# Issuing the DRAM weight sums of both layers earlier in a two-layer attention kernel

## The chip, the cores and the metric

The kernel runs on one core of a Trainium2 chip. The metric is the device time of one execution in microseconds, the median of the runs. The core has TensorE (matrix products), VectorE, ScalarE, GpSimd (called Pool below) and SyncE, each with its own in-order stream of instructions; they meet at semaphores. SyncE and Pool also issue DMA transfers, which run on the core's 16 DMA engines.

## The reference

Two transformer layers in a row, on 512 tokens of width 1024 and 16 meta tokens, in float32. Layer one:

```
proj  = rms_norm(h) @ w_in            # queries, keys, values, latent, index keys, gates
o_a   = sliding-window attention with sinks (8 heads)
o_b   = latent attention: an indexer picks the top 128 keys of each token,
        softmax over them, bias by distance
h    += (sigmoid(gate_a) * (o_a @ w_branch_a) + sigmoid(gate_b) * (o_b @ w_branch_b)) @ w_out
h    += (silu(rms_norm(h) @ w_gate) * (rms_norm(h) @ w_up)) @ w_down      # width 2816
```

Layer two has the same frame; its attentions are a differential attention (4 heads of two softmax maps each) and a windowed attention with grouped keys and sinks. A final rms_norm gives the 512 output rows.

## The kernel before, in words

Every large product is taken in three passes: a weight tile (1024 x 128, 512 KB) is loaded by SyncE into one of two `stage` buffers, ScalarE rounds it to `wh` (L918), and VectorE or Pool subtracts to get the low half `wl` (Pool: `low`, L746); TensorE then multiplies high by high, high by low and low by high. TensorE waits for the low half of a tile before its first product (in `product` and `gate_quarters`), and SyncE loads the next tile into a buffer only when its low half is made.

The work stands in a fixed order on each engine. The stages (`PHASES`) are, in layer one: `kv1`, `bq1`, `iq1`, `aq1`, `uq1` (keys and query weights), `gates1` woven with the window attention and the top-k selection, latent attention, `br1`, `out1`, and the feed-forward in three parts a, b and c: gate/up products `gu1a` (from about 375 us), down products `dn1a` (456), `gu1b` (500), `dn1b` (567), `gu1c` (600), `dn1c` (680). In layer two: `kv2` (730), `qa2`, `qb2`, the differential attention (to 884), `gates2` woven with the window attention, `br2`, `out2`, and the same three feed-forward parts (`gu2a` ends near 1199).

Part of the gate/up products uses a scheme with fewer multiplications: it needs, beside the weights themselves, sums of quarters of the weight matrices. These sums are made in DRAM by Pool's DMAs. `sum_dmas` issues them: for each of the three parts of a layer 16 transfers, the first 8 plain copies (L769), the next 8 accumulating (L771, `accum_op=ALU.add`), of which 8 to 11 take from the weights and 12 to 15 from the sums. A transfer is 512 KB in part a, 768 KB in b, 1024 KB in c. All count on one semaphore, `sums_in`. SyncE waits for a whole part at L672 and then loads the sums (`wsum`) beside the weights.

Before the change Pool issued them so. In `gates1`, two after the low halves of each of 8 pairs of weights (`SUMS_AT[1]`), all of part a. In latent attention, one after every fourth of 32 masks (`mask_bias`, which may run four masks ahead of VectorE), the 8 copies of part b. Then `feed_sums(1)`: when the last mixed tile of layer one is there (`mix_ok`), the accumulates of b and all of part c, each after the landing of the one before. In layer two: one after every second of Pool's 14 steps in the differential attention (`stack_maps_meta`, which copies the meta columns of a map into `m8d`, where TensorE turns them after each 4 maps), copies of part a; one to three after each pair of `gates2`; the rest in `feed_sums(2)`. A wait for the landing of all transfers before stood ahead of steps 0, 8, 12 and 14 of part a and step 0 of part b, and from step 8 of part b on ahead of every transfer; in latent attention and in the differential attention none of them but the first could stop Pool.

Lines that the steps below touch: Pool's waits and copies between the stages (L792 to L904), TensorE's turn of `m8d` (L2529), its gate products (L2520), VectorE's use of a mask (L1697), the ordinary products (L2293) and those with sums (L2316).

## Time and profile before

| | us |
|---|---|
| median of 3 runs | 1472.45 (1471.33 to 1475.7) |
| profiled execution, its own time | 1473.38 |
| its span, first to last instruction | 1471.7 |
| TensorE busy | 1452.7 |
| VectorE / ScalarE / Pool busy | 975.2 / 654.3 / 258.2 |
| mean granted TensorE clock | 0.997 |

A row of a timeline gives the start in us from the span's start, the duration, the engine, the line and the tiles; what stands in brackets is how long the engine was idle before it and what released it. A Pool row with DMA_DIRECT2D is the time in which Pool issues a transfer, not that in which it runs. "DMA to landing" is the time from the issue to the last byte. The clock is TensorE's granted clock as a share of 2.4 GHz.

### The profile page before, as it was taken

The numbers are of one execution on the slowest core, as the hardware profiler recorded it, in microseconds if no ns is written. First come the engines' busy times: TensorE is split into PE (matmuls) and PEld (weight loads), VectorE is DVE, ScalarE is ACT, GpSimd is POOL, SyncE is SP. The second block draws the span as 40 slices with busy tenths as digits, with TensorE's granted clock in tenths as the row PEclk, the third lists the DMA queues.
The fourth block names the chain that finished last, engine by engine and source line by source line (L and its number), as shares of the span: only waits on it lengthen the run. The fifth ranks groups of instructions, "written<-read, shape, count | busy, mean of one in ns | idle before, by whom it ended". The sixth has DMA issues, their size and how long they took to land.

```text
span 1471.7 us, 23871 instructions
## 1 busy us (share of the span) xinstructions
PE 1452.7 (99%) x8712; PEld 1253.2 (85%) x8712; DVE 975.2 (66%) x1779; ACT 654.3 (44%) x1175; POOL 258.2 (18%) x260
## 2 busy tenths in 40 slices
PE   9999999999999999999999999999999999999998
PEld 8868786888898898999899777777888988989997
DVE  6678977575776576787744372434767765867875
ACT  5234446535453353465411373544344533534643
POOL 2024536201101100000003675331011001000000
PEclk9999999999999999999999999999999999999999
DMA  7536674249899993663223237653388999736632
GB/s 187 148 100 211 173 133 130 79 111 191 202 328 226 250 217 98 199 184 106 86 86 86 58 101 162 151 188 80 107 186 226 305 218 242 213 95 195 185 104 93
DMA packets 342909, 236.91 MB, mean 161 GB/s; under 512 B 24729, under 2 KB 322837, under 8 KB 342814
## 3 DMA queue, kind: packets, MB, share of 16 engines
q1 hardware_dynamic: 305518, 152.24, 36.4%
q0 software_dynamic: 37216, 83.27, 24.8%
q8 instruction: 60, 0.98, 0.3%
q14 instruction: 35, 0.29, 0.1%
q10 hardware_dynamic: 80, 0.14, 0.0%
HBM read 233.48 MB, written 81.88 MB: 214 GB/s over the span
## 4 chain that ended last, share of the span: by engine, by line
PE 88%; DMA 6%; DVE 3%; ACT 1%; issue 1%; DVEq 0%; SPq 0%; POOL 0%; ACTq 0%
PE psL L2293 37%; PE psL L2520 12%; PE psS L2316 10%; PE psL L2316 6%; PE psS L2293 5%; PE psT L2316 4%; PE psT L2529 2%; DMA stage<-in_w_ffn_up 1%; DMA stage<-in_w_ffn_gate 1%; DMA stage<-in_w_ff_up 1%; PE psL L2655 1%; PE psS L2836 1%; PE psS L2570 1%; PE psL L2791 1%; PE psS L2814 1%
## 5 line engine op out<-in xcount | busy, mean ns | idle before, releaser
L918 ACT ACTIVATE wh<-stage 128x1024 fp32r<-128x1024 f32 (+3 forms) x211 | 203.6, 965 | 362.1 <-PE psL L2293 199.6
L1398 DVE TENSOR_TENSOR wl<-stage,wh 128x1024 fp32r<-128x1024 f32 (+2 forms) x168 | 183.8, 1094 | 57.7 <-ACT wh L918 57.3
L2293 PE MATMUL psL<-hid,wh 128*128 128x512 f32 x672 | 207.3, 390 | 0.0
L2520 PE MATMUL psL<-hn,wh 128*128 128x512 f32 x496 | 165.0, 414 | 0.8 <-DVE yn L2176 0.8
L2293 PE MATMUL psL<-hn,wh 128*128 128x512 f32 x528 | 165.0, 394 | 0.0
L2293 PEld LDWEIGHTS psL<-hid,wh 128*128 128x128 f32 x672 | 125.6, 188 | 26.2 <-DVE wl L1398 0.6
L2293 PE MATMUL psL<-hid,wl 128*128 128x512 f32 x336 | 130.7, 389 | 0.0
L746 POOL TENSOR_TENSOR wl<-stage,wh 128x1024 fp32r<-128x1024 f32 (+1 forms) x43 | 97.7, 2273 | 172.7 <-ACT wh L918 172.7
L2293 PEld LDWEIGHTS psL<-hn,wh 128*128 128x128 f32 x528 | 97.7, 188 | 23.1 <-issue 3.3
L2520 PEld LDWEIGHTS psL<-hn,wh 128*128 128x128 f32 x496 | 84.5, 189 | 24.5 <-issue 11.1
L2293 PE MATMUL psL<-hn,wl 128*128 128x512 f32 x264 | 102.9, 390 | 0.0
L1901 DVE TENSOR_TENSOR wsl<-wsum,wsh 128x1024 fp32r<-128x1024 f32 x72 | 88.2, 1224 | 22.3 <-ACT wsh L1166 21.4
L2520 PE MATMUL psL<-hn,wl 128*128 128x512 f32 x248 | 97.8, 394 | 0.0
L2316 PE MATMUL psS<-xt,wsh 128*128 128x256 f32 x432 | 80.2, 283 | 0.8 <-ACT part_x L1226 0.8
L2293 PE MATMUL psL<-mix,wh 128*128 128x512 f32 x256 | 79.9, 393 | 0.8 <-DVE wl L1814 0.8
L2293 PE MATMUL psS<-hn,wh 128*128 128x264 f32 x416 | 78.5, 290 | 0.9 <-DVE hn L1845 0.5
L1166 ACT ACTIVATE wsh<-wsum 128x1024 fp32r<-128x1024 f32 x72 | 75.4, 1048 | 5.6 <-DMA wsum<-weight_sums_1g 1.9
L2293 PEld LDWEIGHTS psL<-hid,wl 128*128 128x128 f32 x336 | 63.1, 188 | 13.2
L2028 DVE TENSOR_TENSOR ft<-psL,Rk 128x512 f32<-128x512 f32 x46 | 31.8, 691 | 62.4 <-PE psL L2293 62.4
L2316 PEld LDWEIGHTS psS<-xt,wsh 128*128 128x128 f32 x432 | 67.4, 192 | 1.0 <-ACT part_x L1226 1.0
L2293 PEld LDWEIGHTS psS<-hn,wh 128*128 128x128 f32 x416 | 65.7, 192 | 2.6 <-issue 1.2
L2316 PE MATMUL psS<-xt,wsl 128*128 128x256 f32 x216 | 61.1, 283 | 0.0
(507 smaller groups left out, 3333.0 us busy)
## 6 DMA issues: line engine op xcount, KB each, us to landing
stage<-in_w_in SPq DMA_DIRECT2D x53, 512.0 KB, 4.0
wsum<-weight_sums_1g SPq DMA_DIRECT2D x18, 512.0 KB, 5.2
wsum<-weight_sums_1u SPq DMA_DIRECT2D x18, 512.0 KB, 5.3
wsum<-weight_sums_2g SPq DMA_DIRECT2D x18, 512.0 KB, 4.7
wsum<-weight_sums_2u SPq DMA_DIRECT2D x18, 512.0 KB, 4.5
stage<-in_w_out SPq DMA_DIRECT2D x16, 512.0 KB, 4.7
stage<-in_w_ffn_down SPq DMA_DIRECT2D x32, 256.0 KB, 3.0
stage<-in_w_ff_down SPq DMA_DIRECT2D x32, 256.0 KB, 3.0
```

The lines of the kernel that those rows point to most:

```text
L746: pool.tensor_tensor(wl[:, b, 0:n], stage[:, b, 0:n], wh[:, b, 0:n].bitcast(F32), ALU.subtract).then_inc(lo[b], 1)
L918: act.activation(wh[:, b, 0:n], stage[:, b, 0:n], ACT.Copy).then_inc(hi[b], 1)
L1166: act.activation(wsh[:, cols], wsum[:, cols], ACT.Copy).then_inc(ws_hi, 1)
L1398: v.tensor_tensor(wl[:, b, 0:n], stage[:, b, 0:n], wh[:, b, 0:n].bitcast(F32), ALU.subtract).then_inc(lo[b], 1)
L1901: v.tensor_tensor(wsl[:, cols], wsum[:, cols], wsh[:, cols].bitcast(F32), ALU.subtract).then_inc(ws_lo, 1)
L2028: v.tensor_tensor(ft[:, 2 * b, :], psL[:, b, :], R, ALU.mult).then_inc(upper_ok, 1)
L2293: ins = pe.matmul(dst, w[:, b, k * P:(k + 1) * P], x[:, part, k, c0:c1], start=done_ + n == 0, stop=done_ == kc - 1 and n == 2)
L2316: ins = pe.matmul(dst, w[:, cols], x(part, k), start=not add and k + n == 0, stop=k == KD // 2 - 1 and n == 2, skip_group_check=True)
L2520: ins = pe.matmul(psL[:, b, :], w[:, b, k * P:(k + 1) * P], hn[:, part_, k, META:], start=k + n == 0, stop=k == KD - 1 and n == 2)
L2529: ins = pe.transpose(psT[:, n % 2, m * P:(m + 1) * P], tile[:, col:col + P], ident[:])
L2570: ins = pe.matmul(psS[:, 2 * (i % 2) + 1, h * HD:(h + 1) * HD], PTa[:, u % 2, n * P:(n + 1) * P], avn[:, c, h // 4 * HD:h // 4 * HD + HD], ...
L2655: ins = pe.matmul(psL[:, i % 2, h * HD:(h + 1) * HD], PT[:, n % 4, m * P:(m + 1) * P], vB[:, c, h * HD:(h + 1) * HD], start=h == 0 and m = ...
```

## The change

The same 96 transfers are issued, in the same order and with the same sizes, at other places of Pool's stream. `sum_dmas(l, first, last, one_by_one)` now takes numbers 0 to 47 that run over the three parts of a layer. With `one_by_one` it waits before each transfer for the landing of all before it; without, only before steps 0, 8, 12 and 14 of a part. The places:

- layer one: 0 to 6 one by one behind the transfer of the window bias, ahead of the copy into `cm8`; 7 to 25 in `gates1`; 26 to 31 one by one in latent attention, behind masks 1, 6, 11, 16, 21 and 26; 32 to 47 in `feed_sums(1)`;
- layer two: 0 to 7 one by one when TensorE has reached `dn1b`, 8 to 15 when it has reached `dn1c`; 16 to 21 one by one in `kv2`, behind the `iota`; 22 to 29 one by one in the differential attention; 30 to 42 in `gates2`; 43 to 47 in `feed_sums(2)`.

```diff
--- before.py
+++ after.py
@@ -145,7 +145,7 @@
 SUM_DMAS = 16
-SUMS_AT = {1: (0, 2, 4, 6, 8, 10, 12, 14, 16), 2: (8, 10, 12, 14, 16, 19, 22, 24, 26)}
+SUMS_AT = {1: (7, 10, 12, 14, 16, 19, 22, 24, 26), 2: (30, 32, 34, 36, 38, 40, 41, 42, 43)}
 PHASES = [("kv1", 4, KD, 1), ("bq1", 2, KD, 1), ("iq1", 2, KD, 1), ("aq1", 4, KD, 2), ("uq1", 4, 2, 1),
@@ -749,28 +749,27 @@
                 low(name, i, 0)
                 low(name, i, 1)
-            def sum_dmas(l, part, first, last):
-
-                before = SUM_DMAS * (3 * l - 3 + part)
-                t0, t1 = summed_pairs(part)
-                cols = slice(t0 * P, t1 * P)
-                second = slice((FPAIRS + t0) * P, (FPAIRS + t1) * P)
-                upper, lower = slice(0, D // 2), slice(D // 2, D)
+            def sum_dmas(l, first, last, one_by_one=False):
+
                 for n in range(first, last):
-                    if before + n and (n in (0, 8, 12, 14) or 16 * part + n >= 24):
-                        pool.wait_ge(sums_in, 16 * (before + n))
-                    m = "gu"[n % 2]
+                    before = SUM_DMAS * len(FPARTS) * (l - 1) + n
+                    part, step = divmod(n, SUM_DMAS)
+                    t0, t1 = summed_pairs(part)
+                    cols = slice(t0 * P, t1 * P)
+                    second = slice((FPAIRS + t0) * P, (FPAIRS + t1) * P)
+                    upper, lower = slice(0, D // 2), slice(D // 2, D)
+                    if before and (one_by_one or step in (0, 8, 12, 14)):
+                        pool.wait_ge(sums_in, 16 * before)
+                    m = "gu"[step % 2]
                     w, s12, s43 = w_ffn[l, m], w_sums[l, m, 0], w_sums[l, m, 1]
                     to, src = ((s12[upper, cols], w[upper, second]), (s43[lower, cols], w[upper, cols]),
                                (s12[lower, cols], w[lower, second]), (s43[upper, cols], w[lower, cols]),
                                (s12[upper, cols], w[lower, second]), (s43[lower, cols], w[upper, second]),
-                               (s12[lower, cols], s43[lower, cols]), (s43[upper, cols], s12[lower, cols]))[n // 2]
-                    if n < 8:
+                               (s12[lower, cols], s43[lower, cols]), (s43[upper, cols], s12[lower, cols]))[step // 2]
+                    if step < 8:
                         pool.dma_start(to, src).then_inc(sums_in, 16)
                     else:
                         pool.dma_start(to, src, accum_op=ALU.add).then_inc(sums_in, 16)
-
-
             def copies(row, dram, length, h0, h1):
@@ -789,6 +788,7 @@
             copies(fA_row, fA_dram, LEN_A, 0, NH)
             pool.wait_ge(f_out, 16)
             windows(fA_dram, LEN_A, biasA, NEAR, 0, NH, biasA_in)
+            sum_dmas(1, 0, SUMS_AT[1][0], one_by_one=True)
             pool.wait_ge(key_taken, 2)
             pool.tensor_copy(cm8[:], cT[:, 0:META].unsqueeze(1).broadcast_to([P, NH, META])).then_inc(cm8_ok, 1)
             low_pair("uq1", 0)
@@ -803,7 +803,7 @@
                     low("gates1", i, 1)
                 else:
                     low_pair("gates1", i)
-                sum_dmas(1, 0, SUMS_AT[1][i], SUMS_AT[1][i + 1])
+                sum_dmas(1, SUMS_AT[1][i], SUMS_AT[1][i + 1])
             def mask_bias(j):
@@ -813,11 +813,10 @@
                     pool.wait_ge(ph["la"]["neg"], j - 3)
                 pool.tensor_tensor(biasM[:, j % 4, 0:K], biasB[:, h, NKEY - K:NKEY], selm[:, i, 0:K], ALU.subtract).then_inc(biasM_ok, 1)
-            def feed_sums(l):
+            def feed_sums(l, first):
                 pool.wait_ge(mix_ok, KD * l)
-                sum_dmas(l, 1, 8 if l == 1 else 10, SUM_DMAS)
-                sum_dmas(l, 2, 0, SUM_DMAS)
+                sum_dmas(l, first, SUM_DMAS * len(FPARTS), one_by_one=True)
             la_units = list(latent_units())
             for b in range(2):
@@ -825,15 +824,20 @@
             pool.wait_ge(biasB_in, 4 * 16)
             for j in range(len(la_units)):
                 mask_bias(j)
-                if j % 4 == 3:
-                    sum_dmas(1, 1, j // 4, j // 4 + 1)
-
-            feed_sums(1)
+                if j % 5 == 1 and j < 30:
+                    sum_dmas(1, SUMS_AT[1][-1] + j // 5, SUMS_AT[1][-1] + j // 5 + 1, one_by_one=True)
+
+            feed_sums(1, SUMS_AT[1][-1] + 6)
+            pool.wait_ge(mm[0], PAIR0["dn1b"])
+            sum_dmas(2, 0, 8, one_by_one=True)
+            pool.wait_ge(mm[0], PAIR0["dn1c"])
+            sum_dmas(2, 8, 16, one_by_one=True)
             pool.wait_ge(ev[1], PAIR0["kv2"] + 1)
             pool.memset(m8d[:, :, 4 * META:], 0.0).then_inc(zeros, 1)
             pool.iota(dist[:], pattern=[[-1, DIST]], base=3 * P, channel_multiplier=1,
                       allow_small_or_imprecise_dtypes=True).then_inc(dist_ok, 1)
+            sum_dmas(2, 16, 22, one_by_one=True)
             def bias_unit(j):
@@ -893,13 +897,12 @@
                 else:
                     bias_window(u - 8, u - 7)
                 if u % 2 == 0:
-                    sum_dmas(2, 0, u // 2 - 1, u // 2)
-            sum_dmas(2, 0, 7, 8)
+                    sum_dmas(2, 21 + u // 2, 22 + u // 2, one_by_one=True)
+            sum_dmas(2, 29, 30, one_by_one=True)
             for i in range(PAIRS["gates2"]):
                 low_pair("gates2", i)
-                part = SUMS_AT[2][i] // SUM_DMAS
-                sum_dmas(2, part, SUMS_AT[2][i] - part * SUM_DMAS, SUMS_AT[2][i + 1] - part * SUM_DMAS)
-            feed_sums(2)
+                sum_dmas(2, SUMS_AT[2][i], SUMS_AT[2][i + 1])
+            feed_sums(2, SUMS_AT[2][-1])
         @block.scalar
```

## Rows read from the trace of the kernel before

**Rows 1.** The page, part 1: engine, busy us (share of the span), instructions.

```profile
PE 1452.7 (99%) x8712; PEld 1253.2 (85%) x8712; DVE 975.2 (66%) x1779; ACT 654.3 (44%) x1175; POOL 258.2 (18%) x260
```

**Rows 2.** Windows: stretch, length, then busy us (instructions) by engine, clock, DMA share, GB/s.

```profile
416.00:456.00 40.00, 40.00 (x336) 40.00 (x334) 30.12 (x42) 22.54 (x39) 3.55 (x5) 1.00 0.95 297
500.00:542.00 42.00, 37.79 (x298) 37.18 (x297) 27.02 (x36) 20.95 (x35) 2.95 (x3) 0.96 1.04 248
1157.00:1199.00 42.00, 40.77 (x336) 40.17 (x335) 29.87 (x42) 22.14 (x38) 4.33 (x5) 1.00 1.00 257
```

**Rows 3.** Windows: the stretch behind TensorE's gap.

```profile
516.00:520.00 4.00, 3.67 (x18) 3.68 (x19) 3.90 (x5) 2.80 (x7) 0.00 (x0) 0.57 1.04 175
```

**Rows 4.** Chain of waits, 500 to 545: start us, us, what.

```profile
513.36 11.18 DMA stage<-in_w_ffn_gate
```

**Rows 5.** Timeline of Pool, 40 to 110: start, us, operation, idle before it.

```profile
43.14 0.94 POOL L783 DMA_DIRECT2D biasA<-bias_by_distance_A  x1 [9.38 <-DMA bias_by_distance_A<-bias_row_A]
77.52 0.29 POOL L793 COPY cm<-cT 128x128 f32<-128x128 f32 x1 [33.44 <-DVE ikz L1624]
...
104.16 0.65 POOL L769 DMA_DIRECT2D weight_sums_1g<-in_w_ffn_gate  x1
...
108.39 2.40 POOL L746 TENSOR_TENSOR wl<-stage,wh 128x1024 fp32r<-128x1024 f32 x1 [2.24 <-ACT wh L918]
```

**Rows 6.** Timeline of TensorE: gate product of the second pair of weights.

```profile
115.20 0.73 PE L2520 MATMUL psL<-hn,wh 128*128 128x512 f32 x2
```

**Rows 7.** Line 769, the copies, all 48: time from issue to landing.

```profile
DMA to landing us min/median/max: 4.0/5.6/10.0
```

**Rows 8.** Line 771, the accumulates: all 48, then one in 1010 to 1020.

```profile
DMA to landing us min/median/max: 6.6/8.8/12.3
...
L771 POOL DMA_DIRECT2D weight_sums_2u<-in_w_ff_up x1: 1023/1023/1023, 1015.2 to 1015.2; - x1
...
DMA to landing us min/median/max: 7.0/7.0/7.0
```

**Rows 9.** Timeline of Pool and VectorE in latent attention: masks, then the use of mask 27.

```profile
231.72 0.88 POOL L814 TENSOR_TENSOR biasM<-biasB,selm 128x144 f32<-128x144 f32 x2 [6.62 <-DVE negm L1697]
...
264.16 0.70 DVE L1697 CUSTOM_DVE_ANT_0 W<-psS,biasM 128x528 f32<-128x528 f32 x1
```

**Rows 10.** Timeline of Pool, 320 to 530: first sum transfers of each kind, and the last.

```profile
327.69 1.05 POOL L771 DMA_DIRECT2D weight_sums_1g<-in_w_ffn_gate  x1 [60.38 <-DVE mix L1822]
...
396.07 0.66 POOL L769 DMA_DIRECT2D weight_sums_1g<-in_w_ffn_gate  x1 [8.89 <-DMA weight_sums_1u<-weight_sums_1u]
...
452.18 1.04 POOL L771 DMA_DIRECT2D weight_sums_1g<-in_w_ffn_gate  x1 [6.96 <-DMA weight_sums_1u<-in_w_ffn_up]
...
491.12 1.01 POOL L771 DMA_DIRECT2D weight_sums_1g<-weight_sums_1g  x1 [9.48 <-DMA weight_sums_1u<-in_w_ffn_up]
...
524.66 1.01 POOL L771 DMA_DIRECT2D weight_sums_1u<-weight_sums_1u  x1 [11.60 <-DMA weight_sums_1g<-weight_sums_1g]
```

**Rows 11.** Timeline of Pool in layer two's key products.

```profile
777.94 1.00 POOL L861 COPY vm<-vaT 128x512 f32<-128x512 f32 x1 [34.24 <-DVE vaT L1549]
```

**Rows 12.** Timeline of Pool, end of the differential attention.

```profile
856.29 0.68 POOL L769 DMA_DIRECT2D weight_sums_2g<-in_w_ff_gate  x1
...
880.36 0.21 POOL L852 COPY m8d<-W 128x16 f32<-128x16 f32 x1
...
881.64 0.68 POOL L769 DMA_DIRECT2D weight_sums_2u<-in_w_ff_up  x1
882.34 4.71 POOL L746 TENSOR_TENSOR wl<-stage,wh 128x1024 fp32r<-128x1024 f32 x2
```

**Rows 13.** Timeline of TensorE there: last meta turn, first gate product.

```profile
881.32 0.27 PE L2529 MATMUL psT<-ident,m8d 128*128 128x128 f32 x1
...
884.81 0.70 PE L2520 MATMUL psL<-hn,wh 128*128 128x512 f32 x2 [0.80 <-DVE yn L2176]
```

## The prediction

> **What bounds the kernel now.** I read the page's busy shares first: TensorE is busy for 1452.7 of 1471.7 us [rows 1], so only 19 us of the span is open to a gain, and every microsecond for which TensorE is made to wait is added whole. Then I asked, in windows, where these 19 us lie and whether the moved transfers have to do with them. In 500 to 542 TensorE is busy for 37.8 of 42 us, with a mean clock of 0.96; in 416 to 456, where gate and up products of the same kind run, it is busy throughout, and in 1157 to 1199 it is idle for 1.2 us [rows 2]. The chain of waits in the bad stretch runs over the weight loads: one took 11.2 us from issue to landing [rows 4], and a load and the split behind it have to fit the 10.08 us in which TensorE does half a pair. The Pool timeline says what is different there: from 491.12 on Pool has accumulating transfers in flight, in 416 to 456 plain copies [rows 10]. So accumulates beside gate/up products cost 4.2 us of idle time, and 4 us at clock 0.57 that followed the 2.2 us gap (4 x 0.43 = 1.7 us) [rows 3]: 5.9 us in layer one, 1.2 in layer two. That is all that an earlier start can win directly.
>
> **The change, part by part.** A layer has 48 sum transfers, numbered 0 to 47 here: three parts of 16, in each 8 copies and then 8 accumulates, of 512, 768 and 1024 KB by part. Nothing is added or removed; what changes is when Pool issues each, and where it first waits for the landing of the one before (`one_by_one`). Pool is one in-order engine, so behind such a wait stand its other duties: low halves of weights, masks, stacked meta columns.
>
> *Query weights (0 to 6, before the copy into cm8).* Copies land in 4.0 us at best, 5.6 in the median [rows 7]. Pool is free at 44.1 and has nothing else to do until 77.52 [rows 5]. The first queues behind the bias window transfer, say to 50.6; five more at 4.6 make the seventh issue fall at 73.6. It is hidden; at 5.6 it falls at 78.6, and the low half that counts comes only 6 us after 77.52, so it stays hidden. Cost 0, upper end 2.
>
> *Gates of layer one (7 to 25).* Number 8 waits for 7, which is issued at 104.16. With 4.6 to land, two accumulate issues (1.0 and 1.1) and the bias copy, the next low half starts at about 111.2 instead of 108.39 [rows 5], and is ready at 113.6. TensorE wants it at 115.20 [rows 6]: hidden with 1.6 us to spare. The other waits in this loop are for transfers issued a whole pair, 15 us, earlier. Cost 0, upper end 2.
>
> *Latent attention (26 to 31, 768 KB accumulates).* The price of one accumulate is the heart of this forecast. All 48 of them took 6.6 us at least and 8.8 in the median; the one of this size that ran beside little else took 7.0 [rows 8]. I take 7.0, plus 0.2 to the next issue: a cycle c of 7.2. Number 27 goes out at its natural place, about 232.2 [rows 9]; 28, 29, 30 and 31 follow at c each, the last at 261.0. Its issue (1.0) and the mask of unit 27 (1.2) end at 263.2, and VectorE wants this mask at 264.16 [rows 9]. Hidden by 1.0 us: cost 0. In general it is 4c - 29.8, which is 2.2 us at c = 8.0 and 5.4 at 8.8. The four masks that Pool may run ahead are the cover, and here they are nearly used up.
>
> *Layer one's feed (32 to 47, 1024 KB).* It now starts at 327.7, where mix_ok comes, not at 396.07 [rows 10]. By the rows the 8 copies take 56.1 us, the 4 accumulates from the weights 9.7 each (452.18 to 491.12), the 4 from the sums 11.2 each (491.12 to 524.66 is three). That gives copies to 384, accumulates to 423 and then to 467. So the dear accumulates no longer lie beside the second gate/up stage, but they lie beside the whole of the first one, 416 to 456, with the same loads. The 5.9 us go away in 500 to 542 and come back at 416 to 456. Net 0; the ends are -5.9 (they don't come back) and +3 (some cushion less).
>
> *Layer two's part a (0 to 15) in layer one's down products, and 16 to 21 in the key products.* Copies from 566.7 and accumulates from 680, 512 KB, one at a time, beside loads that leave half of the queues' time free; accumulates end near 738. Pool next stands idle for 34.24 us before 777.94 [rows 11], and six copies need under 34. Cost 0, upper end 1.
>
> *Differential attention of layer two (22 to 29).* Here the old program issued copies without a wait. Now 24 to 29 are 768 KB accumulates, and each waits for the one before. 24 goes out at 856.29 as before [rows 12]; 25 at 863.5, 26 at 870.7, 27 at 877.9, 28 at 885.1, 29 at 892.3. Before, the last was issued at 881.64. Two duties stand behind these waits. The last meta column (880.36 before [rows 12]) comes after 28, at 886.3, and TensorE turns it at 881.32 [rows 13]: a wait of 5.0 us. Then follow 3.5 us of work to 889.8. The low half of the first gate weights starts at 893.3 and is ready 2.4 later [rows 12], at 895.7; TensorE wanted it at 884.81 [rows 13]. Both waits together: 10.9 us. Nothing covers them, since TensorE's order is fixed. After the second wait I add one fall of the clock as in [rows 3], 1.7 us (after the first it is hidden in the second wait). Bounds: with c = 6.8 it is 8.9, with 9.0 it is 19.9; the clock 0 to 3.4.
>
> *Gates and out products of layer two (30 to 47).* Two issues a pair, as before; only five accumulates are left for the feed, so they are done before 1157, and the 1.2 us there [rows 2] are won.
>
> Sum: 10.9 + 1.7 + 0 - 1.2 = +11.4 us. The profiled execution took 1473.38 us (span 1471.7), so it becomes 1484.8; it lies 0.9 above the median of the runs, hence 1484 for the median.
>
> The Trainium skill ("DMA: Bandwidth & Descriptors", section "Anatomy of one DMA — SWDGE (gpsimd) path") puts a transfer issued from GpSimd at about 2.0 us and its bytes over 436 GB/s, 3.8 us for 768 KB. If accumulates obeyed that, no wait would reach TensorE at all. The rows say 7.0 us for such an accumulate [rows 8], so the trace does not bear the rule out for accumulates, though it comes near for copies (4.0 at best [rows 7]).
>
> **The rivals.**
> *A: the accumulates leave layer one's gate/up stages unharmed.* For it: the feed starts 68 us earlier, and if accumulates run faster beside the out products, part of them is over before 416. Against it: 134 us of transfers from 327.7 end after 456 in any case. Full effect -5.9: 1478.
> *B: the cycle is longer, 8.0 us.* For it: the median of 8.8 [rows 8]. Against it: few weight loads run in 846 to 895. Then 5 x 0.8 = 4 us more at the gates and 2.2 us in latent attention: 1490.
> *C: an earlier wait surfaces* in the query weights or at the first gates, where the margins are 1.6 to 6 us: about 3 us more, and a fall of the clock: 1489.
> *D, not slower: accumulates that wait for one another land as fast as copies,* since each has the queues to itself. For it: all accumulates of 512 KB were issued in twos. The point from which it decides: c at most 5.0 (856.3 + 5c + 1.0 + 2.4 under 884.8). Then the gates wait for nothing, the feed is over by about 440, and -1.2 and some 3 of the 5.9 us are won: 1468. Against it: the row of 7.0 us had the queue to itself too, and the minimum of 48 is 6.6.
>
> **How the numbers follow.** My forecast 0.58, A 0.18, B 0.13, C 0.05, D 0.06. The time is the forecast's, 1484. Downwards the range takes in A, 1477; upwards B and a little, 1492. A measurement tells about 0.3% (4.4 us) from no change. Only D is faster (0.04; in a weak form it is no change, 0.02), and A together with a cheap cycle comes to no change with 0.02. That leaves 0.92 for slower.
>
> **What would show it.** Right: Pool's issues 7.2 us apart from 856 on, the last at about 892; TensorE idle for 5 us before its last turn of m8d and again before its first gate product, with a fall of the clock behind it; the same idle pattern as in 500 to 542 now in 416 to 460, and none in 500 to 542 or 1170 to 1210. Wrong: accumulates under 5 us, or idle TensorE in the latent stretch 240 to 270, or at 105 to 116.

## The result and the profile after

The changed kernel takes 1494.51 us (median of 4 runs, 1492.79 to 1494.8) against 1472.08 for the kernel before on the same chip: the ratio is 1.0155, with an interval of 1.0135 to 1.0175. So it is slower by about 22 us where 11.4 were forecast, and it lies above the range. Its profiled execution took 1492.79 us, with a span of 1491.0 us against 1471.7: 19.3 us to explain. The busy shares after:

```profile
PE 1457.9 (98%) x8712; PEld 1255.7 (84%) x8712; DVE 980.1 (66%) x1779; ACT 655.6 (44%) x1175; POOL 258.6 (17%) x260
```

TensorE's idle time rose by only 14.1 us [rows 1]; the rest is the clock. To find where the time went I took each of the 8712 products in both traces and asked how much later it starts, counted from the span's start. All kernels here issue the same products in the same order, so this can be done for each; the marks are times of the kernel before:

```
us later at mark    40   222   262   416   460   500   546   740   880   890   925  1157  1200  1450
changed            0.3   0.3   7.4   7.1  10.3  10.3   3.8   2.2   2.6  16.5  21.5  21.4  19.4  19.4
e1 layer one       2.9   2.9   8.9   8.8   9.2   9.2   2.7   2.6   2.7   2.7   2.7   2.7   2.0   4.7
e2 layer two      -0.2  -0.2  -0.2   0.5   0.5   0.5  -3.7  -5.3  -5.1  11.4  11.4  11.2   9.1   9.1
e3                 2.6   2.6   5.0   5.6   9.2   9.2   2.7   1.2   1.6  15.9  17.0  17.7  15.7  15.7
e4                 1.0   1.0   7.8   7.9  11.2  11.2   4.8   4.8   4.8   8.8  14.8  14.7  12.7  12.7
e5                 1.2   1.2   8.4   8.4  11.4  11.4   5.0   3.4   3.4   9.4   9.5  10.1   8.1   8.1
e6                 0.1   0.1   7.1   7.0   8.7   8.8   2.3   4.1   4.6  18.8  23.4  23.5  21.5  21.4
e7                 2.9   2.9   2.6   2.2   5.0   5.0  -1.5  -1.5  -1.5  -1.8   3.5   4.6   2.5   2.5
e8                 0.8   0.7   7.9   7.8   8.4   8.4   1.9   1.9   2.1  10.0  10.1  10.1   8.1   8.1
e9                -0.1  -0.1  -0.3  -0.6   1.4   1.4  -5.1  -5.2  -5.1  -5.4  -5.4  -5.2  -4.9  -4.9
e10                0.0   0.0   7.3   7.1  10.0  10.0   3.5   1.9   2.7  16.5  16.6  16.8  14.8  14.8
e11                2.4   2.4   2.2   1.8   1.8   1.8   0.4   1.2   2.9  18.4  18.4  19.1  17.1  17.1
e12                1.4   1.3   1.1  12.0  12.0  12.0   5.5   7.1   7.1   6.8   6.8   7.8   9.5   9.4
e13                1.2   8.8  15.4  15.1  17.4  17.4  10.9  12.4  13.2  27.3  28.5  29.2  27.1  27.1
e14                0.2   1.8   8.1   7.9   8.3   8.3   1.8   1.8   1.9  16.8  18.1  17.8  15.8  15.8
```

What stands at mark 40 differs from one execution to the next and lies ahead of every moved transfer. For the changed kernel the steps are: **+7.1 in latent attention (222 to 262), +3.2 in gu1a, -6.5 in gu1b (500 to 546), -1.6 before 740, +13.9 at the end of the differential attention (880 to 890), +5.0 in the first gates of layer two (890 to 925), -2.0 before 1200**. The first and the sixth were not in the forecast. Nor was the -1.6, and it is not the change's: the kernel before runs at a mean clock of 0.57 in 731 to 735, and the changed one at 1.00 in the same stage.

```profile
731.00:735.00 4.00, 4.00 (x22) 4.00 (x22) 3.38 (x21) 1.06 (x1) 0.00 (x0) 0.57 0.42 126
...
733.00:737.00 4.00, 4.00 (x36) 4.00 (x36) 2.62 (x16) 0.65 (x1) 0.00 (x0) 1.00 0.45 131
```

The kernels whose transfers of layer two's part a and in the key products stand as in the changed one range from -1.6 to +1.8 between 546 and 740.

**Latent attention.** Pool's timeline there, the accumulates 27 to 31 and two rows of masks (start, us, operation, idle before):

```profile
234.76 1.01 POOL L772 DMA_DIRECT2D weight_sums_1u<-in_w_ffn_up  x1
...
242.23 1.01 POOL L772 DMA_DIRECT2D weight_sums_1g<-weight_sums_1g  x1 [2.83 <-DMA weight_sums_1u<-in_w_ffn_up]
...
249.76 1.01 POOL L772 DMA_DIRECT2D weight_sums_1u<-weight_sums_1u  x1 [2.95 <-DMA weight_sums_1g<-weight_sums_1g]
250.43 4.88 POOL L814 TENSOR_TENSOR biasM<-biasB,selm 128x400 f32<-128x400 f32 x5
257.10 1.01 POOL L772 DMA_DIRECT2D weight_sums_1g<-weight_sums_1g  x1 [1.80 <-DMA weight_sums_1u<-weight_sums_1u]
```

VectorE's rows in the kernel before (masks 16 and 17), then VectorE's and TensorE's in the changed one:

```profile
248.44 0.57 DVE L1697 CUSTOM_DVE_ANT_0 W<-psS,biasM 128x400 f32<-128x400 f32 x1
...
248.93 0.57 DVE L1697 CUSTOM_DVE_ANT_0 W<-psS,biasM 128x400 f32<-128x400 f32 x1
```

```profile
244.09 0.44 DVE L1700 CUSTOM_DVE_ANT_0 W<-psS,biasM 128x272 f32<-128x272 f32 x1 [2.61 <-POOL biasM L814]
...
248.75 0.56 DVE L1700 CUSTOM_DVE_ANT_0 W<-psS,biasM 128x400 f32<-128x400 f32 x1
251.86 0.57 DVE L1700 CUSTOM_DVE_ANT_0 W<-psS,biasM 128x400 f32<-128x400 f32 x1 [2.54 <-PE psS L2631]
```

```profile
255.48 0.47 PE L2532 MATMUL psT<-ident,m 128*128 128x128 f32 x1 [3.90 <-DVE m L1774]
```

Masks 12 to 16 stand behind the wait for 27's landing, and VectorE waits for mask 12 until 244.09; this was still made up for. Masks 17 to 21 stand behind that for 28's, so 17 is begun only at 250.43. VectorE uses 16 at 248.75 and 17 at 251.86; in the kernel before they followed one another, at 248.44 and 248.93. The row names `psS` as the releaser, but what has moved is the mask, which ended at about 251.4. TensorE stands for 3.90 us and then runs at a lower clock, as the windows show (stretch, length, busy us of TensorE, its weight loads, VectorE, ScalarE and Pool, clock, DMA share, GB/s):

```profile
252.00:262.00 10.00, 6.52 (x29) 5.06 (x30) 6.68 (x16) 4.17 (x12) 7.58 (x9) 0.66 0.79 122
255.50:261.50 6.00, 6.00 (x25) 4.54 (x25) 2.88 (x11) 2.78 (x8) 3.78 (x4) 0.50 0.60 82
416.00:460.00 44.00, 42.30 (x319) 40.30 (x317) 30.49 (x41) 22.29 (x36) 5.02 (x5) 1.00 1.11 263
500.00:546.00 46.00, 46.00 (x346) 44.29 (x346) 34.24 (x45) 23.73 (x38) 0.00 (x0) 1.00 0.63 184
...
896.00:902.00 6.00, 2.36 (x6) 1.93 (x7) 0.00 (x0) 0.00 (x0) 5.77 (x3) 0.53 0.73 110
...
899.60:903.20 3.60, 3.56 (x9) 2.85 (x10) 0.00 (x0) 0.00 (x0) 2.25 (x1) 0.50 1.15 221
912.00:925.00 13.00, 9.90 (x42) 7.46 (x41) 6.38 (x7) 3.96 (x10) 6.36 (x4) 0.87 0.84 206
1157.00:1199.00 42.00, 42.00 (x269) 38.37 (x268) 32.68 (x43) 21.80 (x33) 0.00 (x0) 1.00 0.56 161
```

In 252 to 262 the mean clock is 0.66, but part of that lies in the idle time. Behind the wait, in 255.5 to 261.5, TensorE is busy throughout at half its clock (1.2 GHz), so about 3.0 us are lost to the clock beside the 3.9 us of the wait; the kernel before was busy there throughout. The windows of 416 and 500 answer to [rows 2]: gu1a idles for 1.7 us where it idled for nothing, gu1b no longer idles. The last: gu2a has no gap left.

**End of the differential attention and first gates of layer two.** Pool's timeline (the transfers are 24 to 31 and 33; L772 accumulates, L770 copies):

```profile
858.49 1.09 POOL L772 DMA_DIRECT2D weight_sums_2g<-in_w_ff_gate  x1
...
865.93 1.08 POOL L772 DMA_DIRECT2D weight_sums_2u<-in_w_ff_up  x1 [0.81 <-DMA weight_sums_2g<-in_w_ff_gate]
...
873.49 1.06 POOL L772 DMA_DIRECT2D weight_sums_2g<-in_w_ff_gate  x1 [2.87 <-DMA weight_sums_2u<-in_w_ff_up]
...
881.17 1.06 POOL L772 DMA_DIRECT2D weight_sums_2u<-in_w_ff_up  x1 [3.57 <-DMA weight_sums_2g<-in_w_ff_gate]
...
888.71 1.06 POOL L772 DMA_DIRECT2D weight_sums_2g<-weight_sums_2g  x1 [3.63 <-DMA weight_sums_2u<-in_w_ff_up]
889.39 0.59 POOL L856 COPY m8d<-W 128x16 f32<-128x16 f32 x1
...
896.08 1.08 POOL L772 DMA_DIRECT2D weight_sums_2u<-weight_sums_2u  x1 [4.95 <-DMA weight_sums_2g<-weight_sums_2g]
896.78 5.07 POOL L746 TENSOR_TENSOR wl<-stage,wh 128x1024 fp32r<-128x1024 f32 x2
903.63 1.03 POOL L772 DMA_DIRECT2D weight_sums_2g<-weight_sums_2g  x1 [1.79 <-DMA weight_sums_2u<-weight_sums_2u]
913.27 1.01 POOL L772 DMA_DIRECT2D weight_sums_2u<-weight_sums_2u  x1 [8.61 <-issue]
913.91 5.05 POOL L746 TENSOR_TENSOR wl<-stage,wh 128x1024 fp32r<-128x1024 f32 x2
...
927.38 0.64 POOL L770 DMA_DIRECT2D weight_sums_2u<-in_w_ff_up  x1 [5.97 <-issue]
```

And TensorE's three waits:

```profile
890.03 0.47 PE L2532 MATMUL psT<-ident,m8d 128*128 128x128 f32 x1 [5.98 <-POOL m8d L856]
```

```profile
899.64 1.19 PE L2523 MATMUL psL<-hn,wh 128*128 128x512 f32 x2 [5.46 <-issue]
```

```profile
916.70 1.08 PE L2523 MATMUL psL<-hn,wh 128*128 128x512 f32 x2 [3.10 <-POOL wl L746]
```

The two waits that [rows 13] were to turn into are there, each with its cause on Pool: `m8d` is copied at 889.39, right behind the issue of 28, the low half at 896.78, right behind 29. (The second says "issue": the low half of the first gate weights ended at about 899.3, just ahead of the product.) The third was not foreseen. Transfer 31 stands behind 30 with no semaphore wait of its own, and Pool still doesn't issue it for 8.61 us; 30 took 9.4 us to land, from 903.63 to about 913.0, and 31 goes out 0.3 us later. I call this **the hold**. 33 is held in the same way behind 32, for 5.97 us, at no cost that the marks show.

### The profile page after: what moved, and what is told of

Read it like the earlier page. It is cut to its first block, busy times and chain, and to the rows that moved or that the text cites. A ratio compares the mean times of both kernels' runs of the same rounds, so it can differ in the third digit from the quotient of the medians.

```text
span 1491.0 us, 23873 instructions
## 1 busy us (share of the span) xinstructions
PE 1457.9 (98%) x8712; PEld 1255.7 (84%) x8712; DVE 980.1 (66%) x1779; ACT 655.6 (44%) x1175; POOL 258.6 (17%) x260
## 4 chain that ended last, share of the span: by engine, by line
PE 90%; DMA 4%; DVE 2%; issue 2%; POOL 1%; ACT 1%; DVEq 0%; ACTq 0%; SPq 0%; POOLq 0%
PE psL L2296 38%; PE psS L2319 12%; PE psL L2523 11%; PE psL L2319 7%; PE psT L2319 5%; PE psS L2296 5%; PE psT L2532 2%; PE psS L2839 1%; PE psL L2658 1%; DMA weight_sums_2g<-in_w_ff_gate 1%; DMA weight_sums_2u<-in_w_ff_up 1%; PE psS L2573 1%; PE psS L2817 1%; PE psS L2560 1%; PE psS L2631 1%
```

## The experiments

Each label's kernel is the changed one with the edit shown. A theory's "old places" are those of the kernel before. In the first batch, of e1 to e4, the kernel before took 1470.71 us, in the second, e5 to e8, 1471.5, in the third, e9 to e11, 1472.59, in the last, e12 to e14, 1472.18; each ratio is to these.

**Which layer.** e1: layer two's transfers at their old places. e2: layer one's.

```diff
-SUMS_AT = {1: (7, 10, 12, 14, 16, 19, 22, 24, 26), 2: (30, 32, 34, 36, 38, 40, 41, 42, 43)}
+SUMS_AT = {1: (7, 10, 12, 14, 16, 19, 22, 24, 26), 2: (8, 10, 12, 14, 16, 19, 22, 24, 26)}   # e1
+SUMS_AT = {1: (0, 2, 4, 6, 8, 10, 12, 14, 16), 2: (30, 32, 34, 36, 38, 40, 41, 42, 43)}      # e2
```

> Layer one's transfers at the new places, layer two's at the old ones. Theory (the waits between accumulates are the loss): TensorE waits about 3.9 us in latent attention and loses some 2.6 us to the clock there, the stall of 500 to 542 (4.2 us and 1.7 us of clock) shrinks to about 2.1 us without a fall of the clock at 438 to 461: +2 to +3 us against before, about 1475. Rival (the loss comes with layer two's transfers beside layer one's down products as well): about 1472 here, and more than +20 in the twin kernel.

> Layer two's transfers at the new places, layer one's at the old ones. Theory: three waits of TensorE between 880 and 915 (6.0, 5.5 and 3.1 us) with falls of the clock, and about 2 us won in layer two's feed: +17 to +20 us against before, 1489 to 1492. But layer one's feed then ends at about 536, so nothing else changes. Rival (the two layers' losses are one, through DMA load): +10 or less.

e1 took 1477.03 us, ratio 1.0046 (1.0023 to 1.007); e2 1481.62, ratio 1.0075 (1.0048 to 1.0101). e1's marks show the latent loss again (+6.0 from 222 to 262) and the gain of 6.5 in gu1b; its median lies 6.3 us above the kernel before, where 2 to 3 were expected. e2 was expected 17 to 20 us above and lies 10.9 above, nearly the +10 of its rival: the third wait is not there, and layer one's stages came out faster as well. Together they make 1.2% of the change's 1.55%. The missing 5 us are the size of the hold, which e2 doesn't have, but the intervals of the three ratios are too wide to settle that. The marks settle it for the hold itself: in e2 31 follows 30 at once, and TensorE loses nothing between the marks 890 and 925:

```profile
897.25 1.03 POOL L772 DMA_DIRECT2D weight_sums_2g<-weight_sums_2g  x1 [1.82 <-DMA weight_sums_2u<-weight_sums_2u]
897.90 1.42 POOL L772 DMA_DIRECT2D weight_sums_2u<-weight_sums_2u  x1
```

e2 also warns against reading single microseconds: its layer one is the old one, and yet it gained 4.2 us between 500 and 546. Of the 6.5 us that the changed kernel gained there, one execution can't say how much is the change's.

**Latent attention.** e3 drops the waits one by one there (28 and 30 keep theirs).

```diff
-                    sum_dmas(1, SUMS_AT[1][-1] + j // 5, SUMS_AT[1][-1] + j // 5 + 1, one_by_one=True)
+                    sum_dmas(1, SUMS_AT[1][-1] + j // 5, SUMS_AT[1][-1] + j // 5 + 1)
```

> The changed kernel, but in latent attention Pool waits only before transfers 28 and 30, not before each. Same transfers at the same places. Theory: 28 still goes out at about 242, 29 at 247 instead of 250, so mask 17 is ready 3 us earlier: TensorE's wait falls from 3.9 to about 1 us and the clock does not fall, 5 to 6 us less than the changed kernel, about 1489. Rival (the transfers themselves delay the masks through load on the queues or Pool's issue time): no change, 1494.

1488.0 us, ratio 1.0126 (1.009 to 1.0161). As expected, TensorE waits less and its clock doesn't fall behind this shorter wait, and 2.4 us are lost at 262 instead of 7.1:

```profile
255.05 0.55 PE L2532 MATMUL psT<-ident,W 128*128 128x128 f32 x3 [1.48 <-ACT W L1056]
```

**Differential attention.** e4 drops the waits one by one for 22 to 29 (24 and 28 keep theirs). e5 makes 24 to 29 plain copies at the same places, with the same waits; their additions are left out, so its output is not that of the layers. e8 moves 29, which stands between the loop and the gates, into the first turn of the gates, and the later ones a turn later.

```diff
-                    sum_dmas(2, 21 + u // 2, 22 + u // 2, one_by_one=True)     # e4
-            sum_dmas(2, 29, 30, one_by_one=True)
+                    sum_dmas(2, 21 + u // 2, 22 + u // 2)
+            sum_dmas(2, 29, 30)
...
-                    if step < 8:                                               # e5
+                    if step < 8 or l == 2 and 24 <= n < 30:
...
-            sum_dmas(2, 29, 30, one_by_one=True)                               # e8
-SUMS_AT = {1: ..., 2: (30, 32, 34, 36, 38, 40, 41, 42, 43)}
+SUMS_AT = {1: ..., 2: (29, 30, 32, 34, 36, 38, 40, 42, 43)}
```

> The changed kernel, but in layer two's differential attention Pool waits only before transfers 24 and 28. Theory: 24 to 27 go out at their natural places, only 28 waits, till about 887; the last meta column is then 3 us late instead of 6, the gate weights' low half about 3 to 4 instead of 12.6: 10 to 14 us less than the changed kernel, 1481 to 1485. Rival (the DMA engines are the limit there, five accumulates at 5 us each): the waits only move to 28, and it stays within 4 us of the changed kernel, 1490 or more.

> The changed kernel, but transfers 24 to 29 of layer two are plain copies with the same places, sizes and waits (the additions of these six are left out of the computation). Theory (the stall is five times the landing of an accumulate, and a copy of 768 KB lands in about 4.9 us): Pool is held until about 884 at most, both waits of TensorE before the gates vanish, 13 to 14 us less than the changed kernel. If the third wait (3.1 us and 1.7 us of clock) comes from transfer 31 alone it stays: about 1480; otherwise about 1476. Rival (the wait is in the one-by-one form or the added traffic, not in the kind of transfer): 1490 or more.

> The changed kernel, but transfer 29 of layer two goes out alone in the first turn of the gates instead of ahead of their low halves, and the later ones one turn later. Theory (each accumulate waited for ahead of the low halves costs its cycle of 7.5 us): TensorE's 6.0 us wait for the last meta column stays, that for the first gate weights nearly goes (5.5 to under 1 us, and the fall of the clock is then no longer hidden): 5 to 7 us less than the changed kernel, and no third wait if 31 is not held: 1484 to 1489. Rival (the delay is set by the load of the DMA engines up to there): no change, 1494.

e4: 1486.32 us, 1.0111 (1.0083 to 1.0138). e5: 1481.13, 1.006 (1.0037 to 1.0083). e8: 1486.47, 1.0104 (1.0064 to 1.0143). Pool's issues of 28 and 29 in e5, and TensorE's first gate product:

```profile
883.08 0.68 POOL L770 DMA_DIRECT2D weight_sums_2g<-weight_sums_2g  x1
888.32 0.68 POOL L770 DMA_DIRECT2D weight_sums_2u<-weight_sums_2u  x1 [3.23 <-DMA weight_sums_2g<-weight_sums_2g]
```

```profile
891.48 1.19 PE L2523 MATMUL psL<-hn,wh 128*128 128x512 f32 x2 [4.07 <-issue]
```

With copies nobody waits for `m8d`: a copy lands in 4.6 to 5.0 us, and Pool stands for none of 24 to 27 before it issues the next. One wait for 29 is left, since 28 had been issued just before. The 13.9 us at the end of the loop become 6.0. In e8, where the low half stands behind no transfer, the gates wait for nothing and only `m8d` is late:

```profile
890.39 0.48 PE L2531 MATMUL psT<-ident,m8d 128*128 128x128 f32 x1 [6.82 <-POOL m8d L856]
```

7.9 us are left of 13.9. In e4 4.0 are left. So each wait is the in-order landing of accumulates ahead of Pool's duty, as forecast. (e4 was expected at 1481 to 1485, a little less than measured; e5 at about 1476 where 31 is not held, because both waits were to go and one is left; e8 is within its 1484 to 1489.) What e4 wins there it gives back in part: its hold of 6.44 us costs 6.0 us between 890 and 925, that of 8.61 in the changed kernel 5.0.

**The hold.** Two theories: Pool runs out of room for a transfer's descriptors at a fixed place of the sequence; or it depends on what else is in flight. e6 shifts the sequence by one more copy of 512 KB (it also waits for this copy ahead of latent attention).

```diff
             sum_dmas(1, 0, SUMS_AT[1][0], one_by_one=True)
+            pool.dma_start(spare, w_ffn[1, "g"][0:D // 2, 0:2 * P]).then_inc(spare_in, 16)
```

> The changed kernel with one more copy of 512 KB, into a spare tensor, behind transfer 6 of layer one, where Pool is idle. It asks why transfers 31 and 33 of layer two, which have no wait of their own, went out only when 30 and 32 had landed. Theory (a place in Pool's list of descriptors, set by all that Pool has issued since the start): the hold moves to other transfers or vanishes, and with it the third wait of TensorE near 916: 4 to 5 us less, 1490. Rival (31 and 33 are held by what runs beside them): they are held as before, 1494 to 1495.

1497.36 us, 1.0169 (1.013 to 1.0207). The hold stayed, 9.1 us for 31, with 4.6 us between the marks 890 and 925: a shift by one copy doesn't move it, and the theory in this form fell. Then one transfer a turn in the gates (e10), the seven copies of the query weights undone (e11), the seven without waits (e13), and six of them instead of seven (e14):

```diff
-SUMS_AT = {1: (7, 10, 12, 14, 16, 19, 22, 24, 26), 2: (30, 32, 34, 36, 38, 40, 41, 42, 43)}
+SUMS_AT = {1: (7, 10, 12, 14, 16, 19, 22, 24, 26), 2: (30, 31, 32, 33, 34, 35, 36, 37, 38)}   # e10
+SUMS_AT = {1: (0, 2, 4, 6, 8, 10, 12, 14, 16), 2: (30, 32, 34, 36, 38, 40, 41, 42, 43)}       # e11
+SUMS_AT = {1: (6, 9, 12, 14, 16, 19, 22, 24, 26), 2: (30, 32, 34, 36, 38, 40, 41, 42, 43)}    # e14
...
-            sum_dmas(1, 0, SUMS_AT[1][0], one_by_one=True)                                     # e11
...
-            sum_dmas(1, 0, SUMS_AT[1][0], one_by_one=True)                                     # e13
+            sum_dmas(1, 0, SUMS_AT[1][0])
```

> The changed kernel with nothing else altered than layer two's gates: one transfer a turn (30 to 37), the other ten in the feed. Theory (hold of the second transfer of a turn): the two waits at the end of the differential attention stay (about 13 to 14 us), the third, 5.0 us between 890 and 925, goes: 1494.5 - 5 = 1489.5. Rival (hold bound to the time, not to the second transfer): 1494.5. Rival (the gates' low half waits for accumulates however they are issued): no change either, with TensorE idle before 917.

> The changed kernel without the seven transfers in the query weights: layer one's gates carry 0 to 15 as in the kernel before, latent attention 16 to 21 (copies of 768 KB, one by one, in the changed kernel's places), the feed starts at 22. Layer two as changed. Theory on latent attention (the price is the landing time of an accumulate behind a one-by-one wait): copies of 768 KB land in about 5 us, so the masks are not late and the 7.1 us of 250 to 262 go, while the feed has four transfers more to do and lies longer in gu1b, as before (the 3.3 us won in layer one go too): 1494.5 - 7.1 + 3.3 = 1491. On the hold in layer two's gates: if it is the earlier query transfers of layer one that set it, transfer 31 is not held here and 5 us more are won, 1486; if not, it is held for about 8 us at 904 to 913 as in the changed kernel. Rival on latent attention (the wait itself, not the accumulate, is what costs): 7 us stay at 250 to 262, 1498.

> The changed kernel with the seven transfers in the query weights issued back to back instead of one by one; everything else as changed. A look at the hold of transfer 31 in layer two's gates (8.61 us in the changed kernel, none in e11_query_undone, where these seven stand in the gates). If the order of Pool's transfers is what sets it (the seven ahead of the bias window of the second half and of its row copies), it is held here too, 8 to 9 us, and TensorE loses about 5 us between 890 and 925. If it is the waits one by one that set it, 31 follows 30 by 0.7 us. The time is otherwise that of the changed kernel, 1489 to 1495.

> The changed kernel with six instead of seven transfers in the query weights (the seventh goes to the first turn of gates1, which then issues three, as does the second). If the hold of transfer 31 hangs on how many transfers stand ahead of the others, it moves to another transfer of layer two's gates or goes away; if it hangs only on there being early ones, 31 is held for 8 to 9 us again. The time is otherwise that of the changed kernel, 1489 to 1495.

e10: 1492.26 us, 1.0152 (1.011 to 1.0194), from runs 13 us apart, so the time itself tells nothing; its profile does. 31 is issued without a hold and TensorE loses 0.1 us instead of 5.0:

```profile
917.18 1.00 POOL L772 DMA_DIRECT2D weight_sums_2u<-weight_sums_2u  x1
```

e11: 1488.0 us, 1.0108 (1.0074 to 1.0142), where 1486 was expected without a hold. No hold either, with two transfers a turn:

```profile
904.87 1.03 POOL L772 DMA_DIRECT2D weight_sums_2g<-weight_sums_2g  x1 [1.68 <-DMA weight_sums_2u<-weight_sums_2u]
905.52 1.42 POOL L772 DMA_DIRECT2D weight_sums_2u<-weight_sums_2u  x1
```

e13 (one run, 1500.51 us) and e14 (one run, 1489.12) have it again, 6.72 and 6.50 us, at a cost of 1.2 and 1.3 us between 890 and 925. The price of a hold is what Pool's next low half is late, not its length: 7.12 us cost 0.1 in e8, 6.44 us cost 6.0 in e4. Over all kernels, the hold is there (on 31 and 33 in the changed one, e3, e4, e6, e7, e8, e13 and e14, on 33 and 37 in e5), and each time the held transfer goes out 0.2 to 0.3 us after the one before has landed. Three things meet there: early copies in the query weights, six or seven, with or without waits; layer two's transfers at their new places; and two of them in a turn.

Where one of the three is missing it is not seen, but this says less than it seems to. In e10 (and e9 and e12 below) the gates' transfers without a wait go out 2.7 us or more after the one before has landed, so a hold could not show: they show what it cost, not that it is gone. In e1 31 has a wait of its own, but there the gates' second transfers are not held (23 follows 22 after 0.62 us), and they are earlier ones of the sequence. In e2 and e11, which also change what latent attention and the feed carry, Pool's transfers follow one another in the order of the kernel before; e13 keeps the changed order, drops the waits, and is held. That speaks for the order of the sequence and against the waits. A place in Pool's list of descriptors that depends on this order is not excluded by e6's one copy, and no run tests it. The cause stays open. VectorE is busy for only 1.7 of the 8.6 us held, and no fetch of instructions falls into the hold of 31 in any kernel.

e11 has a second answer: latent attention then carries copies with the very same waits, and nothing is lost there (-0.2 by mark 262, TensorE's longest idle 0.34 us). It is the accumulate's landing time behind a wait that costs; the wait alone (e11) and accumulates without waits (e7 below) cost nothing. e13 and e14 show how thin the cover was at the start. Issued back to back, the seven copies make TensorE wait (7.6 us by mark 100, which is why e13 lies above its expected 1489 to 1495), and one transfer more in the first turn of the gates costs 1.6 us by mark 222:

```profile
69.67 1.19 PE L2296 MATMUL psL<-hn,wh 128*128 128x512 f32 x2 [5.11 <-DVE iqT L1556]
```

```profile
116.95 0.73 PE L2523 MATMUL psL<-hn,wh 128*128 128x512 f32 x2 [1.49 <-POOL wl L746]
```

**Versions that should keep the gain without the waits.** e7: latent attention issues its accumulates in pairs behind masks 3, 15 and 31, the differential attention 25 to 27 at u = 8, 12 and 14 without waits one by one, and the gates take 28 on. e9 is e7 with one transfer a turn in the gates. e12 is e9 with layer one's feed not waiting for `mix_ok`.

```diff
-                if j % 5 == 1 and j < 30:                                      # e7
-                    sum_dmas(1, SUMS_AT[1][-1] + j // 5, SUMS_AT[1][-1] + j // 5 + 1, one_by_one=True)
+                if j in (3, 15, 31):
+                    first = SUMS_AT[1][-1] + 2 * (3, 15, 31).index(j)
+                    sum_dmas(1, first, first + 2)
...
-                pool.wait_ge(mix_ok, KD * l)                                   # e12
+                if l == 2:
+                    pool.wait_ge(mix_ok, KD * l)
```

> A version without Pool's waits in the two attentions: in latent attention the six accumulates go out in pairs behind masks 3, 15 and 31; in layer two's differential attention 22 to 27 go out at steps where nothing has to be waited for, and 28 to 42 in the gates. All else as in the changed kernel. Theory: the losses of 6.9 and 13.9 us go, the third wait too unless a transfer is held there; what is left are the gains in the feeds (3 to 6 us in layer one, 2 in layer two): 2 to 8 us faster than before, 1464 to 1469. Rival (moving transfers forward costs by itself, by load on the queues): as before or slower, 1472 or more.

> The kernel of e7_no_held_masks, but behind each of the 8 pairs of gate weights of layer two Pool issues one weight-sum transfer (28 to 35) instead of one or two (28 to 42); the other twelve (36 to 47) follow one by one in the feed. Theory: the second transfer of a turn, which waits for no semaphore, is held by Pool until the one before it has landed (8.80 and 6.90 us in e7_no_held_masks), and this held the low halves of the next pair back: TensorE idle 3.43 us before 914 and 5.3 us lost with the clock's fall. With one transfer a turn nothing can be held, all of the 5.3 us come back, and twelve transfers of about 10 us in the feed are over by about 1140, before gu2a's last loads: 1474.6 - 5.3 = 1469 us, ratio to before 0.9975. Rival (the hold belongs to a moment of the run, not to the second transfer of a turn): one of the single transfers is held too, or the low halves wait otherwise in 890 to 925: 1474 to 1475. A second price, if it shows: the feed runs later into gu2a, 1 to 3 us of idle TensorE before 1200.

> The kernel of e9_one_a_turn, but the feed of layer one (32 to 47, 1024 KB) doesn't wait for the last mixed tile: it begins when Pool has issued 31, at about 268 instead of 327, where Pool otherwise stands idle for 58.73 us. Theory (what costs in layer one is accumulates that run beside gate/up products, wherever these stand): 8 copies of about 7 us and 8 accumulates of about 10 end near 405, before gu1a starts to load at its full rate; both dear stretches are then free: the 2.0 us that e9_one_a_turn still loses between 416 and 460 go, so 1466.7 - 2.0 = 1464.7 of span, a median of about 1468.5, ratio 0.997 to 0.998. Rival (transfers of 1024 KB beside the weights of br1 and out1 cost there what they cost in gu1a, since these stages load every weight tile too): 2 to 5 us of new idle TensorE between 268 and 400, ratio 1.000 to 1.002.

e7: 1474.56 us, 1.001 (0.999 to 1.003), where 1464 to 1469 was expected. Latent attention costs nothing (-0.3), nor does the end of the differential attention (-0.3), but 31 is held for 8.80 us and costs 5.3. e9: 1470.73 us, 1.0005 (0.9981 to 1.003); no hold shows, its profiled span is 1466.7, 5.0 us under the kernel before. But its 12 runs lie between 1465.19 and 1484.44, those of the kernel before between 1465.18 and 1475.8, so the runs don't show it faster. TensorE's only idle time where the change had three waits:

```profile
879.38 0.70 PE L2526 MATMUL psL<-hn,wh 128*128 128x512 f32 x2 [0.49 <-DVE yn L2182]
```

e12: 1477.92 us, 1.0043 (1.0023 to 1.0062); here my theory fell and the rival held, at twice its price of 2 to 5 us. The accumulates are gone from 416 to 460, and so is what they cost there (0.0), but 10.9 us are lost between 262 and 416. The windows of the kernel before, then of e12, and a row of TensorE in it:

```profile
262.00:330.00 68.00, 67.59 (x367) 55.94 (x367) 43.27 (x82) 29.14 (x56) 5.52 (x6) 1.00 0.33 100
330.00:416.00 86.00, 86.00 (x382) 70.20 (x381) 59.13 (x84) 39.02 (x52) 9.62 (x11) 1.00 0.94 214
```

```profile
262.00:330.00 68.00, 64.68 (x354) 52.21 (x353) 39.80 (x78) 26.92 (x55) 12.78 (x15) 1.00 0.75 210
330.00:416.00 86.00, 81.25 (x351) 65.47 (x350) 55.36 (x81) 36.35 (x49) 7.06 (x7) 0.98 0.91 190
```

```profile
342.12 0.90 PE L2300 MATMUL psL<-mix,wh 128*128 128x512 f32 x2 [4.07 <-DVE wl L1405]
```

Of the 10.9 us, 5.1 are lost by mark 330, where the kernel before had a DMA share of only 0.33, beside the copies: this share did not mean that a second stream could run there for nothing. The other 5.8 come between 330 and 340, beside the first accumulate of 1024 KB.

## Why the prediction was wrong, step by step

- **Latent attention, forecast 0, measured 7.1: this step failed.** The step took the waits to be hidden by 1.0 us. It tested one mask, that of unit 27, behind the last transfer. But each of the waits holds masks back, and the tight one was that for 28's landing, ahead of mask 17. Two inputs were off too: 27 went out at 234.76 and not at 232.2 (the row of 231.72 is masks 4 and 5, not 6 [rows 9]), and the cycle was 7.3 to 7.5 us, not 7.2. What stood there instead is a wait of TensorE of 3.9 us and half the clock behind it. The cost is shown: e11 (same waits, copies) and e7 (pairs without them) lose nothing, e3 loses 2.4. "Idle TensorE in the latent stretch" was named as the sign of an error, and it was one.
- **End of the differential attention, forecast 10.9 + 1.7, measured 13.9: right.** The cycles were 7.44, 7.56, 7.68, 7.54 and 7.37 us, not 7.2, which makes 37.6 us for the five instead of 36.0; 24 went out at 858.49, not 856.29, but everything stands 2.2 to 2.6 us later by then. Hence 29 at 896.08 instead of 892.3, and waits of 5.98 and 5.46 us. e5 and e8 take one of the two away each, and 6.0 and 7.9 us are left. TensorE runs at half its clock behind both waits. The first fall is hidden in the second wait, as forecast; the second costs 1.8 us (half the clock in 899.6 to 903.2), where 1.7 were forecast.
- **Gates of layer two, forecast 0, measured 5.0: this step failed too.** "Two issues a pair, as before" took an issue without a semaphore wait to be free. The hold made it wait for the landing before. e10 and e11, without a held transfer, lose 0.1 and 0.0 there. Why it is held is not known.
- **Layer one's feed, forecast 0, measured -3.3:** gu1a lost 3.2 instead of 5.9, and gu1b won 6.5 instead of 5.9. The timing was right: the last accumulate went out at 457.45, to land near 467. So rival A held in part. Every kernel in which the feed begins with 32 gains 6.4 or 6.5 there, while the loss in gu1a is anything from 0.4 to 3.6 among them (and 0.0 in e12, whose accumulates are over by then). But e2 gains 4.2 with the old order, so the size is not settled. (The prediction's 134 us for the feed are 139.7 by its own terms; 132 were measured, and either end lies behind 456.)
- **Query weights, gates of layer one, part a in the down and key products, forecast 0:** measured 0.0, 0.0 (marks 40 to 222) and -1.6, the last by the clock of the kernel before near 731. Right, with the thin margin at the gates that e14 shows.
- **gu2a, forecast -1.2, measured -2.0.** Right. It goes when twelve transfers are left to the feed (e9 +0.3, e12 +1.7), not with ten (e10 -2.0).

By the table's marks: 0.3 + 7.1 - 0.3 + 3.2 - 6.5 - 1.6 + 0.4 + 13.9 + 5.0 - 0.1 - 2.0 = 19.4, of a span 19.3 us longer. Rival B's cycle of 8.0 us did not come; its 2.2 us in latent attention were nearer than my 0 for the wrong reason. D is out: the cycle of accumulates of 768 KB was never under 7.3 us in the changed kernel. The 4.0 us that the prediction sets beside the price of a 768 KB transfer is that of a 512 KB copy; copies of 768 KB landed in 4.6 to 5.0 us (e5). The medians differ by 3.1 us more than the profiled spans do (22.4 against 19.3); that is within what executions of one kernel differ by here.

## What to carry to other kernels

A wait for a transfer on an in-order engine costs what the engine's next duties are late, and each such wait in a loop has to be tested against its own next duty: here the tightest was not the last. A low DMA share alone did not make room for moved traffic (e12); of the 19 us that stood open here, the best of these versions recovered 5.0 in one profile and nothing that the runs can tell. An issue of a transfer is not free because it waits for no semaphore: one a turn, issued when the one before had landed, was never held here.

## What the runs showed of the hardware

- An accumulate from DRAM to DRAM of 768 KB, one at a time, repeats every 7.3 to 7.7 us in the two attentions of the changed kernel; a copy of the same size every 5.0 to 5.3 where the wait decides (e5, e11).
- Pool can hold a second transfer that waits for no semaphore until the one before has landed: 8.61 and 5.97 us in the changed kernel, 5.7 to 9.1 in eight others. Second transfers of a turn in the gates of e2 and e11 follow after 0.65 us; the kernels differ only in where transfers stand. The trace shows it as idle time released by "issue".
- Beside idle times of TensorE of 3.1 to 6 us in the changed kernel the granted clock was half for some microseconds, 0.50 in 255.5 to 261.5 and in 899.6 to 903.2. In latent attention this cost 3.0 us beside a wait of 3.9; e3's wait of 1.48 us at the same place brought no fall.
